# Gate logits computed with standing weights and a moving token tile, in the cross-attention stage of a one-layer decoder kernel

## The chip, the cores and the metric

The program runs on one core of a Trainium2 chip. The metric is the device time of one execution in microseconds; less is better. The core has a matrix engine (TensorE, in the profile PE, with its weight loads as PEld), VectorE (DVE), ScalarE (ACT), GpSimd (POOL) and a queue engine for transfers (SyncE, SP). Each engine works through its own instructions in program order; semaphores join them.

## The reference, cut to what matters

One decoder layer over 2048 tokens of width 1024: token mixing, cross-attention over 256 memory tokens with 4 heads, and a mixture of experts. This case touches the end of the cross-attention part, where the residual stream `x` is normalised and the experts' gate reads it:

```python
x = x + memory_cross_attention(rmsnorm(x, norm_cross), rmsnorm(mem, norm_mem), ...)
h = rmsnorm(x, norm_moe)
g_logits = h @ w_group + b_group      # 2048 x 4
e_logits = h @ w_router + b_router    # 2048 x 32
# top-1 group by g_logits, then top-2 experts of that group by e_logits
```

The 36 logits of a token decide which experts it goes to, so they are computed to float32 accuracy, not to the reduced accuracy of the chip's fast 4-byte mode (`F32R`). Large products elsewhere in the kernel split both operands into a high and a low `F32R` part and take three products (`split_product`, L62 to 66).

## The kernel before, in words

`attend_memory` handles the cross-attention of all 16 tiles of 128 tokens. It first folds the projections into the keys and values (8 steps, `wq_t`, `sk_hi`, `sk_lo`, `vo_hi`, `vo_lo`); then it runs rounds `b` from -2 to 16, software-pipelined over the tiles. The loop in the middle holds two rounds in its body and turns four times; the first five and the last six rounds are written out. `there(b, lag)` says whether tile `b + lag` exists.

In a round `b` TensorE does, in this order: the scores of tile b+1 (`z_ps`, 48 matmuls of 512 columns, L64 to 66); the transposes of the normalised tile b-1 (`turn_hm`, into `s_ps`, L1587); the transposes of tile b+2 of the input (`turn_x`, into `h_ps`); the output of tile b (`x_ps`, 48 matmuls); the gate logits of tile b-1 (L1668); the transposes of the attention weights of tile b+1 (`s_ps`, L1587). In round 15 (`is_last`) `turn_hm` stands behind the output instead of ahead of it. The logits of before are 8 float32 matmuls in which the transposed token tile `hm_t` (128 x 128) is the standing operand and the gate's weights `w_logit` (128 x 36) move:

```python
pe.wait_ge(mt_out, b)
for r in range(rows):
    last = nc.tensor.matmul(h_ps[:, 0, 0:n_logit], hm_t[:, r], w_logit[:, r], ...)
last.then_inc(logit_done, 1)
```

ScalarE in a round: high part of the transposed attention weights (L1458), square of the residual for the norm (L1464), square of a later input tile (L1426), copy of the transposed tile `hm_t` (L1471), high part of the input (L1432), four exponentials (L1480).

VectorE in a round: residual add (L1539, into `x2_sb`), low part of the attention weights (L1544, `p_lo`), norm of tile b-1 (L1548, L1552, which writes `hm_sb`), norm of a later tile (L1490, L1492), row maximum (L1558), low part of the input (L1503), softmax division (L1565, L1568), and last the logits' bias add (L1578), which writes `logits`. In round 15 `picks.choose(nc, link, 0, 14)` (L1711 on) stands ahead of that bias add: it chooses group and experts for tiles 0 to 13. In round 16 `picks.choose(nc, link, 14, 1)` does so for tile 14, again ahead of the bias add. The last tile is chosen for in the next stage, which begins after a barrier of all engines (`Scope.close`, L28 to 31).

Of the kernel before, what the change touches and what calls it, by code (L numbers as in the profile page):

```python
# [14 lines left out]
P = 128  # L15
# [1233 lines left out]
class CrossLoads:  # L1249


    def __init__(self, s, w_q, w_o):
        self.w_q, self.w_o = w_q, w_o
        self.xs = s.sbuf("cross_xs", [P, 2, w_q.shape[1]])
        self.work = s.sbuf("cross_work", [P, 4, w_q.shape[1]])
        self.wq_loaded = [s.sem(f"wq_loaded{i}") for i in range(2)]
        self.wo_loaded = [s.sem(f"wo_loaded{i}") for i in range(2)]
# [14 lines left out]

def attend_memory(nc, x1, gain_q, ahead, key_t, value_t, gain_moe, w_group, w_router, b_group, b_router,
                  ident, half, x2, hm, logits, consts):
# [13 lines left out]
    with ExitStack() as stack:  # L1288
# [14 lines left out]
        p_sb, x2_sb, hm_sb = work[:, 0], work[:, 1], work[:, 2]  # L1303
        hm_t = work[:, 3].rearrange("p (r t) -> p r t", t=P)
        p_hi, p_lo = p_parts[:, 0], p_parts[:, 1]
# [12 lines left out]
                 "res_loaded x2_stored hm_stored squared meaned rooted h_done ht_done hh_done hl_done scored maxed negated exped "  # L1318
                 "inverted p_done tp_done ph_done pl_done xo_done added m_squared m_meaned m_rooted hm_done tm_done mt_out "
                 "logit_done logit_out picked")  # L1320
        (consts_loaded, gains_loaded, wt_done, wt_act, wt_dve, sk_done, sk_cut, sk_ready, vo_done, vo_cut, vo_ready,
         res_loaded, x2_stored, hm_stored, squared, meaned, rooted, h_done, ht_done, hh_done, hl_done, scored, maxed, negated, exped,
         inverted, p_done, tp_done, ph_done, pl_done, xo_done, added, m_squared, m_meaned, m_rooted, hm_done, tm_done, mt_out,
         logit_done, logit_out, picked) = (s.sem(n) for n in names.split())
        halves = [slice(0, rows // 2), slice(rows // 2, rows)]
# [16 lines left out]
        def is_first(b):  # L1342

            return isinstance(b, int) and b == -2

        def there(b, lag):

            return not isinstance(b, int) or 0 <= b + lag < tiles

        with nc.Block() as block:  # L1350
# [44 lines left out]
            @block.gpsimd  # L1395
            def _(pool):
                def root(t):
                    pool.wait_ge(meaned, t + 1)
                    nc.gpsimd.tensor_tensor(stat[:, 2:3], stat[:, 1:2], half[:, 0:1], ALU.pow).then_inc(rooted, 1)

                root(0)

                def step(b, slot):
                    if there(b, -1):
                        pool.wait_ge(m_meaned, b)
                        nc.gpsimd.tensor_tensor(m_stat[:, 2:3], m_stat[:, 1:2], half[:, 0:1], ALU.pow).then_inc(m_rooted, 1)
                    if there(b, 3):
                        root(b + 3)

                rounds(pool, step)  # L1410

            @block.scalar
            def _(act):
# [39 lines left out]
                def step(b, slot):  # L1453
# [11 lines left out]
                    if there(b, 3):  # L1465
                        square(b + 3, 1 - slot, (b + 3) // 2 + 1)
                    if there(b, -1):
                        act.wait_ge(tm_done, b)
                        wait_past(act, logit_done, b - 1)
                        for cut in halves:  # L1470
                            last = nc.scalar.copy(hm_t[:, cut], s_ps[:, cut])  # L1471
                        last.then_inc(mt_out, 1)
                    if there(b, 2) and not is_first(b):
                        high_x(b + 2)
                    if there(b, 1):
                        act.wait_ge(negated, b + 2)
                        wait_past(act, tp_done, b + 1)
                        for h in range(heads):
                            cut = slice(h * slots, (h + 1) * slots)
                            last = nc.scalar.activation(p_sb[:, cut], z_ps[:, cut], ACT.Exp,  # L1480
                                                        bias=soft_stat[:, 1, h:h + 1], scale=scale, accum_out=soft_stat[:, 2, h:h + 1])
                        last.then_inc(exped, 1)

                rounds(act, step)

            @block.vector
            def _(dve):
# [46 lines left out]
                def step(b, slot):  # L1534
# [19 lines left out]
                    if there(b, 3):  # L1554
                        norm(b + 3, 1 - slot)
                    if there(b, 1):
                        dve.wait_ge(scored, b + 2)
                        nc.vector.tensor_reduce(soft_stat[:, 0], z_ps[:].rearrange("p (h m) -> p h m", h=heads), AX.X, ALU.max).then_inc(maxed, 1)  # L1558
                        dve.wait_ge(maxed, b + 2)
                        nc.vector.tensor_scalar(soft_stat[:, 1], soft_stat[:, 0], -scale, None, ALU.mult).then_inc(negated, 1)  # L1560
                    if there(b, 2) and not is_first(b):
                        low_x(b + 2)
                    if there(b, 1):
                        dve.wait_ge(exped, b + 2)
# [11 lines left out]
                    if there(b, -1):  # L1576
                        dve.wait_ge(logit_done, b)
                        nc.vector.tensor_tensor(logits[:, bass.ds(b - 1, 1), :], h_ps[:, 0:1, 0:n_logit],  # L1578
                                                b_logit[:].rearrange("p (o c) -> p o c", o=1), ALU.add).then_inc(logit_out, 1)
# [4 lines left out]
            def _(pe):  # L1584
# [16 lines left out]
                for n in range(rows):  # L1601
# [22 lines left out]
                    last.then_inc(vo_done, 1)  # L1624
                pe.wait_ge(consts_loaded, 80)

# [6 lines left out]
                def step(b, slot):  # L1633
# [27 lines left out]
                    if there(b, -1):  # L1661
                        pe.wait_ge(mt_out, b)
                        if there(b, 2):
# [3 lines left out]
                        for r in range(rows):  # L1667
                            last = nc.tensor.matmul(h_ps[:, 0, 0:n_logit], hm_t[:, r], w_logit[:, r], start=r == 0, stop=r == rows - 1)  # L1668
                        last.then_inc(logit_done, 1)
                    if there(b, 1):  # L1670
# [3 lines left out]
                        pe.wait_ge(p_done, b + 2)  # L1674
                        wait_past(pe, mt_out, b)
                        transposes(s_ps, p_sb, tp_done)

                rounds(pe, step)
# [698 lines left out]
def build_trunk(nc, x, mem, norm_mix, w_in, v_norm, w_spatial, b_spatial, out_norm_a, out_norm_b, w_out, norm_cross, norm_mem,  # L2377
# [16 lines left out]
    with ExitStack() as stack:  # L2394
# [8 lines left out]
        with ExitStack() as before_moe:  # L2403
# [15 lines left out]
            with ExitStack() as crossing:  # L2419
                c = Scope(nc, crossing, "kv")  # L2420
                key_t, value_t = c.sbuf("key_t", [P, rows, slots]), c.sbuf("value_t", [P, rows, slots])
                ahead = CrossLoads(c, w_xq[0], w_xo[0])
                project_memory(nc, memory, w_xk[0], w_xv[0], ident[:], consts, key_t, value_t, ahead, tiles)
                picks = attend_memory(nc, x1, norm_cross[0], ahead, key_t, value_t, norm_moe[0], w_group[0], w_router[0],
                              b_group[0], b_router[0], ident[:], half, x2, hm, logits, consts)
# [27 lines left out]
```

## Time and profile before

| what | value |
|---|---|
| median of 3 runs | 2663.56 us (2662.22 to 2663.6) |
| profiled execution, first to last instruction | 2659.8 us |
| TensorE busy | 2536.7 us (95% of the span) |
| VectorE busy | 1478.0 us (56%) |
| ScalarE busy | 1283.6 us (48%) |
| GpSimd busy | 602.4 us (23%) |
| mean granted TensorE clock | 0.981 |
| the rounds in the middle | 1300 to 1662 us of the span |
| the last two rounds | 1662.7 to 1696.1 us |

The span of the profiled execution is 3.8 us below the median of the timed runs; this is what lies around the first and last instruction. Busy times of TensorE overlap from one instruction to the next, so what a matmul costs in a stream is read from the distance of two starts, not from its own duration. The granted clock is 1.00 at 2.4 GHz and 0.50 at 1.2 GHz.

### The profile page before, as it was taken

Reading aid. Unit: us, or ns where it says so; the run is one execution under the profiler, and the core shown is the slowest. Engines: PE = TensorE matmul, PEld = TensorE weight load, DVE = VectorE, ACT = ScalarE, POOL = GpSimd, SP = SyncE. Lnnn points to the kernel's source line nnn. Section 1 sums busy time; section 2 is a strip of 40 time slices with the busy share of each in tenths; the row PEclk is TensorE's granted clock in tenths of the full one; section 3 lists DMA queues with packets and bytes.
Section 4 is the critical chain, followed back from the end, with each engine's and each line's share of the span. In section 5 each row is a group of like instructions: output and inputs, shape, how many; then the busy total and the mean of one; then the engine's idle time right before and its main releaser. Section 6 shows DMA issues by size and latency. Waiting matters only on the chain. (4 is left out here: it accounts for less than half of the span.)

```text
span 2659.8 us, 44805 instructions
## 1 busy us (share of the span) xinstructions
PE 2536.7 (95%) x14537; PEld 2053.6 (77%) x14539; DVE 1478.0 (56%) x1943; ACT 1283.6 (48%) x2286; POOL 602.4 (23%) x650
## 2 busy tenths in 40 slices
PE   9999999999999999989999999799999999999991
PEld 7888888676666678886888888688877888888881
DVE  5221344698888964444333332667888655565643
ACT  5221211698898931133222222346787645465543
POOL 0000011577777710000000000012222221121223
PEclk9999999999999999999999999799999999999996
DMA  7433240313201033243122121538999765576757
GB/s 267 167 119 127 75 166 25 100 45 144 65 18 45 2 127 111 99 152 112 62 82 85 73 87 48 200 130 326 386 379 367 267 220 200 191 279 205 253 161 271
DMA packets 141439, 414.83 MB, mean 156 GB/s; under 512 B 22016, under 2 KB 30720, under 8 KB 140288
## 3 DMA queue, kind: packets, MB, share of 16 engines
q1 hardware_dynamic: 125040, 371.15, 37.5%
q0 software_dynamic: 13968, 33.59, 5.3%
q10 hardware_dynamic: 2304, 8.39, 0.8%
q8 instruction: 81, 1.33, 0.2%
q14 instruction: 46, 0.38, 0.0%
HBM read 338.60 MB, written 91.75 MB: 162 GB/s over the span
## 5 line engine op out<-in xcount | busy, mean ns | idle before, releaser
L673 POOL TENSOR_TENSOR stick_weight<-stick_weight,stick_left 128x512 f32<-128x512 f32 (+3 forms) x320 | 327.8, 1038 | 126.9 <-DVE stick_left L805 122.4
L1820 DVE TENSOR_TENSOR moe_w_lo<-moe_w_lo_raw,moe_w_hi (+1 forms) x256 | 298.2, 1220 | 59.6 <-ACT moe_w_hi L1816 53.3
L1816 ACT CAST moe_w_hi<-moe_w_lo_raw (+1 forms) x256 | 255.7, 1052 | 48.2 <-DMA moe_w_lo_raw<-in_w 24.8
L805 DVE TENSOR_TENSOR_SCAN stick_left<-stick_z_ps,stick_left,stick_any_row 128x512 f32<-128x512 f32 x192 | 240.2, 1274 | 35.4 <-ACT stick_z_ps L768 35.1
L766 ACT ACTIVATE stick_weight<-stick_z_ps 128x512 f32<-128x512 f32 (+3 forms) x320 | 173.9, 543 | 32.8 <-PE stick_z_ps L715 21.1
L728 PE MATMUL stick_t_ps<-all_ident,stick_weight 128*128 128x128 f32 x1088 | 165.1, 281 | 19.0 <-ACT stick_weight_t L775 9.2
L768 ACT ACTIVATE stick_z_ps<-stick_z_ps 128x512 f32<-128x512 f32 (+3 forms) x320 | 165.7, 518 | 10.2
L728 PEld LDWEIGHTS stick_t_ps<-all_ident,stick_weight 128*128 128x128 f32 x1088 | 115.9, 141 | 70.0 <-issue 46.2
L64 PE MATMUL exp_g_ps<-moe_w_hi,exp_x_hi 128*128 x376 | 153.1, 407 | 7.1 <-DVE exp_x_lo L2224 7.1
L1831 POOL DMA_INDIRECT moe_xg<-hm_scratch,moe_now x50 | 62.4, 1247 | 412.6 <-PE exp_x_ps L2260 273.7
L64 PE MATMUL proj_z_ps<-proj_w_hi,proj_h_hi 128*128 128x512 f32 x384 | 151.9, 396 | 2.5 <-DVE proj_h_lo L392 2.5
L64 PE MATMUL exp_y_ps<-moe_w_hi,exp_h_hi 128*128 128x512 f32 x376 | 152.1, 405 | 2.3 <-DVE exp_h_lo L2244 2.3
L2248 DVE TENSOR_TENSOR moe_w_lo<-moe_w_lo_raw,moe_w_hi 128x1024 f32 (+1 forms) x128 | 148.2, 1218 | 9.8 <-ACT moe_w_hi L2210 9.8
L66 PE MATMUL proj_z_ps<-proj_w_hi,proj_h_lo 128*128 128x512 f32 x384 | 150.3, 391 | 0.0
L65 PE MATMUL proj_z_ps<-proj_w_lo,proj_h_hi 128*128 128x512 f32 x384 | 150.2, 391 | 0.0
L65 PE MATMUL exp_g_ps<-moe_w_lo,exp_x_hi 128*128 x376 | 148.9, 396 | 0.0
L66 PE MATMUL exp_g_ps<-moe_w_hi,exp_x_lo 128*128 x376 | 148.8, 396 | 0.0
L66 PE MATMUL exp_u_ps<-moe_w_hi,exp_x_lo 128*128 x376 | 148.5, 395 | 0.0
L66 PE MATMUL exp_y_ps<-moe_w_hi,exp_h_lo 128*128 128x512 f32 x376 | 148.5, 395 | 0.0
L64 PE MATMUL exp_u_ps<-moe_w_hi,exp_x_hi 128*128 x376 | 148.3, 394 | 0.0
L65 PE MATMUL exp_u_ps<-moe_w_lo,exp_x_hi 128*128 x376 | 148.3, 394 | 0.0
L65 PE MATMUL exp_y_ps<-moe_w_lo,exp_h_hi 128*128 x376 | 148.2, 394 | 0.0
(290 smaller groups left out, 5820.2 us busy)
## 6 DMA issues: line engine op xcount, KB each, us to landing
moe_w_lo_raw<-in_w SPq DMA_DIRECT2D x384, 512.0 KB, 13.0
proj_w_lo_raw<-in_w_in SPq DMA_DIRECT2D x40, 256.0 KB, 6.3
proj_xs<-in_x SPq DMA_DIRECT2D x16, 512.0 KB, 4.3
qt_scratch<-proj_qk_out SPq DMA_DIRECT2D x16, 512.0 KB, 2.8
kt_scratch<-proj_qk_out SPq DMA_DIRECT2D x16, 512.0 KB, 2.7
mix_q<-qt_scratch SPq DMA_DIRECT2D x16, 512.0 KB, 3.8
mix_out_xs<-in_x SPq DMA_DIRECT2D x16, 512.0 KB, 4.4
x_scratch<-mix_out_xs SPq DMA_DIRECT2D x16, 512.0 KB, 3.0
```

The lines of the kernel that those rows point to most:

```text
L64: pe.matmul(out, left_hi, right_hi, start=first, stop=False)
L65: pe.matmul(out, left_hi, right_lo, start=False, stop=False)
L66: return pe.matmul(out, left_lo, right_hi, start=False, stop=last)
L673: nc.gpsimd.tensor_tensor(taken, taken, after, ALU.mult).then_inc(weight_done, 1)
L728: last = nc.tensor.transpose(t_ps[:, n % 2, b], weight[:, n % W_SLOTS, b * P:(b + 1) * P], ident)
L766: nc.scalar.activation(weight[:, n % W_SLOTS, 0:keys], z, ACT.Sigmoid).then_inc(take_done, 1)
L768: nc.scalar.activation(z, z, ACT.Sigmoid, scale=-1.0).then_inc(leave_done, 1)
L805: nc.vector.tensor_tensor_scan(row[:, c * BANK:c * BANK + keys][:, ::-1], back, any_row[:, 0:keys], start, ALU.mult, ALU.bypass).then_inc( ...
L1816: nc.scalar.copy(self.w13_hi[:, self.w13_at(e, i)], self.w13_raw[:, self.w13_at(e, i)]).then_inc(self.w13_cut, 1)
L1820: ops.tensor_tensor(self.w13_lo[:, self.w13_at(e, i)], self.w13_raw[:, self.w13_at(e, i)], as_f32(self.w13_hi[:, self.w13_at(e, i)]), ALU. ...
L1831: nc.gpsimd.indirect_dma_start(out=self.xg[:], out_offset=None, in_=self.hm, in_offset=bass.IndirectOffsetOnAxis(ap=self.now[:].bitcast(U3 ...
L2248: nc.vector.tensor_tensor(w2_lo[:, w2_at(e, i)], w2_raw[:, w2_at(e, i)], as_f32(w2_hi[:, i]), ALU.subtract).then_inc(w2_ready, 1)
```

## The change

The gate's weights become the standing operand and the token tile moves. For that the weights are split once into a high and a low `F32R` part that stand side by side (`w_cut`, 72 columns), the transposed tile is split into a high and a low part (`hm_parts`, ScalarE and VectorE), and 8 `F32R` matmuls move both parts at once (256 columns) and give all four partial products, transposed (`h_ps[0:72, 1:3]`). ScalarE copies these to `parts`, as its last step of the round; then two float32 matmuls against a 72 x 36 matrix of two stacked identities (`both_parts`, set up by GpSimd ahead of everything) add the products up and turn them back to tokens by logits, where the bias add finds them. The two matmuls stand behind the transposes of the attention weights, as TensorE's last step of the round.

On VectorE the new low part stands between `low_x` and the softmax division, so ahead of `picks.choose` in rounds 15 and 16. The weights are split in round -1: ScalarE waits there for the constants and makes the high part, VectorE the low part. TensorE's wait for the constants ahead of the rounds goes, one for `both_parts` takes its place. `hm_parts` lies over the keys' buffer, `w_cut` and `parts` over the fourth slice of `work`, where `hm_t` was. The core of the diff:

```diff
@@ GpSimd, ahead of the rounds
+                nc.gpsimd.memset(both_parts[:], 0.0).then_inc(both_set, 1)
+                for part in range(2):
+                    pool.wait_ge(both_set, part + 1)
+                    nc.gpsimd.affine_select(out=both_parts[:], in_=both_parts[:], compare_op=ALU.not_equal, fill=1.0, base=-part * n_logit,
+                                            pattern=[[-1, n_logit]], channel_multiplier=1).then_inc(both_set, 1)
@@ ScalarE, a round
+                    if is_early(b):
+                        act.wait_ge(consts_loaded, 80)
+                        nc.scalar.copy(w_cut[:, :, 0:n_logit], w_logit[:]).then_inc(w_hi_cut, 1)
                     if there(b, -1):
                         act.wait_ge(tm_done, b)
                         wait_past(act, logit_done, b - 1)
                         for cut in halves:
-                            last = nc.scalar.copy(hm_t[:, cut], s_ps[:, cut])
+                            last = nc.scalar.copy(hm_parts[:, cut, 0], s_ps[:, cut])
                         last.then_inc(mt_out, 1)
...
+                    if there(b, -1):
+                        act.wait_ge(logit_done, b)
+                        wait_past(act, parts_added, b - 1)
+                        nc.scalar.copy(parts[:], h_ps[0:2 * n_logit, 1:3]).then_inc(parts_out, 1)
@@ VectorE, a round
+                    if is_early(b):
+                        dve.wait_ge(w_hi_cut, 1)
+                        nc.vector.tensor_tensor(w_cut[:, :, n_logit:], w_logit[:], as_f32(w_cut[:, :, 0:n_logit]), ALU.subtract).then_inc(w_cut_done, 1)
...
                     if there(b, 2) and not is_first(b):
                         low_x(b + 2)
+                    if there(b, -1):
+                        dve.wait_ge(mt_out, b)
+                        wait_past(dve, logit_done, b - 1)
+                        for cut in halves:
+                            last = nc.vector.tensor_tensor(hm_parts[:, cut, 1], s_ps[:, cut], as_f32(hm_parts[:, cut, 0]), ALU.subtract)
+                        last.then_inc(ml_out, 1)
...
                     if there(b, -1):
-                        dve.wait_ge(logit_done, b)
+                        dve.wait_ge(parts_added, b)
                         nc.vector.tensor_tensor(logits[:, bass.ds(b - 1, 1), :], h_ps[:, 0:1, 0:n_logit],
@@ TensorE
-                pe.wait_ge(consts_loaded, 80)
+                pe.wait_ge(both_set, 3)
...
-                        pe.wait_ge(mt_out, b)
+                        if isinstance(b, int) and b == 1:
+                            pe.wait_ge(w_cut_done, 1)
+                        pe.wait_ge(ml_out, b)
...
-                            last = nc.tensor.matmul(h_ps[:, 0, 0:n_logit], hm_t[:, r], w_logit[:, r], start=r == 0, stop=r == rows - 1)
+                            last = nc.tensor.matmul(h_ps[0:2 * n_logit, 1:3], w_cut[:, r], hm_parts[:, r], start=r == 0, stop=r == rows - 1)
                         last.then_inc(logit_done, 1)
...
                         pe.wait_ge(p_done, b + 2)
-                        wait_past(pe, mt_out, b)
+                        wait_past(pe, ml_out, b)
                         transposes(s_ps, p_sb, tp_done)
+                    if there(b, -1):
+                        pe.wait_ge(parts_out, b)
+                        for part in range(2):
+                            last = nc.tensor.matmul(h_ps[:, 0, 0:n_logit], parts[:, part], both_parts[:], start=part == 0, stop=part == 1)
+                        last.then_inc(parts_added, 1)
```

## Rows read from the trace of the kernel before

**Rows 1.** The page's first line: span and instructions.

```profile
span 2659.8 us, 44805 instructions
```

**Rows 2.** Busy time by stretch; behind POOL: granted clock, DMA share, GB/s.

```profile
1300.00:1662.00 362.00, 362.00 (x1872) 308.17 (x1871) 120.26 (x199) 94.87 (x242) 14.28 (x26) 1.00 0.21 76
```

**Rows 3.** Timeline of a round's end: start, length, engine, line, what, idle before.

```profile
1504.50 1.87 PE L1668 MATMUL cross_h_ps<-cross_w_logit,kv_cross_work 128*128 128x36 f32 x16
...
1506.20 1.07 PE L1587 MATMUL cross_s_ps<-all_ident,kv_cross_work 128*128 128x128 f32 x8
1506.52 0.20 DVE L1578 TENSOR_TENSOR pre_logits<-cross_h_ps,cross_b_logit 128x36 f32 x1 [8.27 <-PE cross_h_ps L1668]
...
1507.03 0.48 PE L64 MATMUL cross_z_ps<-cross_sk_hi,cross_h_hi 128*128 128x512 f32 x1
1507.04 1.29 DVE L1539 TENSOR_TENSOR kv_cross_work<-cross_x_ps,kv_cross_work 128x512 f32<-128x512 f32 x2 [0.33 <-issue]
```

**Rows 4.** Timeline of TensorE where the memory tokens are projected (256 columns).

```profile
1150.01 0.28 PE L64 MATMUL mem_z_ps<-mem_m_hi,mem_w_hi 128*128 128x256 f32 x1
1150.13 0.28 PE L65 MATMUL mem_z_ps<-mem_m_lo,mem_w_hi 128*128 128x256 f32 x1
```

**Rows 5.** Timeline of TensorE in token mixing (weights of 64 columns).

```profile
701.71 1.09 PE L743 MATMUL stick_o_ps<-stick_weight_t,stick_v_other 128*64 128x128 f32 x16
```

**Rows 6.** Groups of instructions on ScalarE by form: count, busy us, mean ns.

```profile
L775 ACT COPY stick_weight_t<-stick_t_ps 128x256 f32<-128x256 f32 x16 | 6.1, 380 | 0.0
```

**Rows 7.** Timeline of VectorE late in the round that ends with rows 3.

```profile
1494.99 1.29 DVE L1503 TENSOR_TENSOR cross_h_lo<-cross_h_ps,cross_h_hi 128x512 fp32r<-128x512 f32 x2 [1.53 <-ACT cross_h_hi L1432]
...
1497.03 1.23 DVE L1568 TENSOR_TENSOR kv_cross_work<-kv_cross_work,cross_soft_stat 128x1024 f32<-128x1024 f32 x1
```

**Rows 8.** Timeline of ScalarE in round -1.

```profile
1268.45 1.07 ACT L1432 CAST cross_h_hi<-cross_h_ps 128x512 fp32r<-128x512 f32 x2 [5.83 <-PE cross_h_ps L1587]
```

**Rows 9.** Timeline of VectorE in round -1.

```profile
1267.58 1.23 DVE L1558 TENSOR_REDUCE cross_soft_stat<-cross_z_ps 128x4 f32<-128x1024 f32 x1 [3.36 <-PE cross_z_ps L66]
```

**Rows 10.** Timeline of VectorE, rounds 15 and 16 and the next stage.

```profile
1668.12 0.21 DVE L1724 TENSOR_REDUCE cross_pick_g_max<-pre_logits 128x14 f32<-128x56 f32 x1
...
1678.39 0.39 DVE L1744 TENSOR_TENSOR cross_pick_both<-cross_pick_pick 128x448 bf16<-128x448 bf16 x1
1684.26 0.20 DVE L1578 TENSOR_TENSOR pre_logits<-cross_h_ps,cross_b_logit 128x36 f32<-128x36 f32 x1 [5.48 <-PE cross_h_ps L1668]
1684.37 1.28 DVE L1539 TENSOR_TENSOR kv_cross_work<-cross_x_ps,kv_cross_work 128x512 f32<-128x512 f32 x2
...
1688.89 0.15 DVE L1724 TENSOR_REDUCE cross_pick_g_max<-pre_logits 128x1 f32<-128x4 f32 x1
...
1693.17 0.17 DVE L1744 TENSOR_TENSOR cross_pick_both<-cross_pick_pick 128x32 bf16<-128x32 bf16 x1
1695.90 0.20 DVE L1578 TENSOR_TENSOR pre_logits<-cross_h_ps,cross_b_logit 128x36 f32<-128x36 f32 x1 [2.56 <-PE cross_h_ps L1668]
1697.52 0.16 DVE L1724 TENSOR_REDUCE cross_pick_g_max<-pre_logits 128x1 f32<-128x4 f32 x1 [1.42 <-PEq L31]
```

**Rows 11.** Timeline of TensorE, rounds 15 and 16.

```profile
1666.25 0.80 PE L64 MATMUL cross_x_ps<-cross_vo_hi,cross_p_parts 128*128 128x512 f32 x1 [2.49 <-DVE cross_p_parts L1544]
...
1679.75 0.40 PE L66 MATMUL cross_x_ps<-cross_vo_hi,cross_p_parts 128*128 128x512 f32 x1
1679.98 1.04 PE L1587 MATMUL cross_s_ps<-all_ident,kv_cross_work 128*128 128x128 f32 x8
1682.18 1.98 PE L1668 MATMUL cross_h_ps<-cross_w_logit,kv_cross_work 128*128 128x36 f32 x16 [1.16 <-ACT kv_cross_work L1471]
1689.03 1.97 PE L1587 MATMUL cross_s_ps<-all_ident,kv_cross_work 128*128 128x128 f32 x8 [4.87 <-DVE kv_cross_work L1552]
1692.16 3.63 PE L1668 MATMUL cross_h_ps<-cross_w_logit,kv_cross_work 128*128 128x36 f32 x16 [1.16 <-ACT kv_cross_work L1471]
```

**Rows 12.** Busy time by stretch in round 15, columns as in rows 2.

```profile
1666.00:1670.00 4.00, 3.75 (x9) 2.98 (x10) 3.10 (x11) 0.00 (x0) 0.55 (x1) 0.50 0.35 137
```

More of the change, by code:

```diff
@@ L1254, in __init__ @@
         self.xs = s.sbuf("cross_xs", [P, 2, w_q.shape[1]])
+        self.work_at = s.next_at()
         self.work = s.sbuf("cross_work", [P, 4, w_q.shape[1]])
@@ L1270, in load_first, with attend_memory @@
             self.load_wo(sp, n)
-def attend_memory(nc, x1, gain_q, ahead, key_t, value_t, gain_moe, w_group, w_router, b_group, b_router,
+def attend_memory(nc, x1, gain_q, ahead, key_t, value_t, key_at, gain_moe, w_group, w_router, b_group, b_router,
                   ident, half, x2, hm, logits, consts):
@@ L1303, in attend_memory @@
         p_sb, x2_sb, hm_sb = work[:, 0], work[:, 1], work[:, 2]
-        hm_t = work[:, 3].rearrange("p (r t) -> p r t", t=P)
+        hm_parts = s.over("hm_parts", [P, rows, 2, P], F32R, key_at)
+        w_cut = s.over("w_cut", [P, rows, 2 * n_logit], F32R, ahead.work_at + 4 * 3 * width)
+        parts = s.over("parts", [2 * n_logit, 2, P], F32, ahead.work_at + 4 * (3 * width + 2 * rows * n_logit))
+        both_parts = s.sbuf("both_parts", [2 * n_logit, n_logit])
         p_hi, p_lo = p_parts[:, 0], p_parts[:, 1]
@@ L1318, in attend_memory @@
                  "res_loaded x2_stored hm_stored squared meaned rooted h_done ht_done hh_done hl_done scored maxed negated exped "
-                 "inverted p_done tp_done ph_done pl_done xo_done added m_squared m_meaned m_rooted hm_done tm_done mt_out "
-                 "logit_done logit_out picked")
+                 "inverted p_done tp_done ph_done pl_done xo_done added m_squared m_meaned m_rooted hm_done tm_done mt_out ml_out "
+                 "logit_done logit_out picked both_set w_hi_cut w_cut_done parts_out parts_added")
         (consts_loaded, gains_loaded, wt_done, wt_act, wt_dve, sk_done, sk_cut, sk_ready, vo_done, vo_cut, vo_ready,
          res_loaded, x2_stored, hm_stored, squared, meaned, rooted, h_done, ht_done, hh_done, hl_done, scored, maxed, negated, exped,
-         inverted, p_done, tp_done, ph_done, pl_done, xo_done, added, m_squared, m_meaned, m_rooted, hm_done, tm_done, mt_out,
-         logit_done, logit_out, picked) = (s.sem(n) for n in names.split())
+         inverted, p_done, tp_done, ph_done, pl_done, xo_done, added, m_squared, m_meaned, m_rooted, hm_done, tm_done, mt_out, ml_out,
+         logit_done, logit_out, picked, both_set, w_hi_cut, w_cut_done, parts_out, parts_added) = (s.sem(n) for n in names.split())
         halves = [slice(0, rows // 2), slice(rows // 2, rows)]
@@ L1344, in is_first, with is_early @@
             return isinstance(b, int) and b == -2
+        def is_early(b):
+            return isinstance(b, int) and b == -1
         def there(b, lag):
@@ L2420, in build_trunk @@
                 c = Scope(nc, crossing, "kv")
+                key_at = c.next_at()
                 key_t, value_t = c.sbuf("key_t", [P, rows, slots]), c.sbuf("value_t", [P, rows, slots])
@@ L2423, in build_trunk @@
                 project_memory(nc, memory, w_xk[0], w_xv[0], ident[:], consts, key_t, value_t, ahead, tiles)
-                picks = attend_memory(nc, x1, norm_cross[0], ahead, key_t, value_t, norm_moe[0], w_group[0], w_router[0],
+                picks = attend_memory(nc, x1, norm_cross[0], ahead, key_t, value_t, key_at, norm_moe[0], w_group[0], w_router[0],
                               b_group[0], b_router[0], ident[:], half, x2, hm, logits, consts)
```

## The prediction

> **What bounds the kernel now.** I read the first line of the page for the span [rows 1], then the busy time by stretch, then timelines of single rounds engine by engine. In the middle rounds TensorE is busy for 362.00 of 362 us at full clock [rows 2]: whatever shortens its stream there shortens the kernel by as much, and nothing that the other engines do counts until TensorE waits for it. At the end of the stage it is the other way round. In rounds 15 and 16 TensorE idles 2.49, 1.16, 4.87 and 1.16 us [rows 11], and the end is set by a chain that goes from engine to engine. All later work starts behind a barrier: the next stage's first VectorE instruction comes 1.42 us after the last bias add [rows 10], and what delays that add delays everything behind it.
>
> So the change has two prices: what a middle round gains on TensorE, and what the last two rounds lose or gain on the chain.
>
> **A middle round on TensorE.** The old logits start at 1504.50 and the transposes behind them at 1506.20 [rows 3]: 1.70 us for 16 records (each float32 matmul leaves two), 0.106 us each. The new eight move 256 columns in the fast mode. Their nearest row is the projection of the memory tokens, the same mode and width, with starts 0.12 us apart [rows 4]: 8 x 0.12 = 0.96 us. Their weights have 72 columns and not 128; 16 matmuls with weights of 64 columns take 1.09 us in all, so some 0.07 us each at most [rows 5], and such loads don't slow the stream. The two float32 matmuls that add up the parts have weights of 128 columns and 36 moving ones, as the old ones have: 4 records x 0.106 = 0.42 us. New sum 1.38 us, against 1.70: a middle round gets 0.32 us shorter, if TensorE never waits.
>
> Bounds: were each of the twelve new records at 0.106 us or below, down to the 0.07 us of [rows 5] for the four small ones, the round would gain 1.70 - 0.85 - 0.28 = 0.57 us; with a wait as below it gains nothing. I take 0.32, since the rows for it have the same shape and mode.
>
> The FP8 and Floating Point Precision page of the Trainium skill (TensorE Precision Notes) says that true float32 takes four passes through the array, which speaks against this change: an old block that paid for its moved columns alone would take 8 x 36 x 4 columns, 0.48 us at 2.4 GHz as an estimate, and the new eight with their 2048 columns 0.85 us. By that rule each round would lose. The row disagrees: the old block takes 1.70 us [rows 3]. The page TensorE: Matmul & The Clock Gate of the Trainium skill (LDWEIGHTS) has the reason: a weight load takes its columns divided by 1.2 ns, 107 ns for 128 columns, and the 0.106 us of a record agrees.
>
> **Does TensorE wait for the parts?** Counted from the start of the eight: the last starts at 0.84 and ends 0.28 later [rows 4], at 1.12. ScalarE is done with its exponentials long before. The old logits end at 1506.37 (1504.50 + 1.87) and release VectorE's bias add at 1506.52 [rows 3], 0.15 us later; with as much the copy starts at 1.27. It is 72 x 256 from PSUM; the 128 x 256 copy takes 0.38 us [rows 6]. The parts are there at 1.65, or at 1.55 if the release takes less. TensorE's transposes start at 0.96 and take until the next matmul 0.83 us (1506.20 to 1507.03 [rows 3]): it comes to its wait at 1.79. The cover is 0.15 to 0.25 us, and it must hold TensorE's own release too. It is thin, and where the loop turns (four times) an engine that has run dry (VectorE in [rows 3]) needs 0.33 us to issue again. If the cover fails, TensorE loses what is missing in each of 14 rounds; 0.3 us each is my bound, worked out as a copy that starts or ends half a copy late plus a share of that issue time.
>
> **The other engines in a middle round.** VectorE gets a low part of the size of `h_lo`: 1.29 us [rows 7]. It stands ahead of the division, which ended at 1498.26 and would end by 1499.6 [rows 7]; TensorE takes its result at 1506.20 and the low part itself at 1504.50 [rows 3]. More than 5 us of cover each, free. The bias add now comes behind the parts, so the residual add starts 0.2 to 0.5 us later than at 1507.04, and what follows from it (norm, transposes, both stores and the next load of the residual by SP's queue) is needed a good 10 us later. Free. ScalarE's cast in place of its copy has the same size, and ScalarE waits for TensorE at the round's end anyway.
>
> **The start.** ScalarE idles 5.83 us in round -1 ahead of its high part, VectorE 3.36 us ahead of its maximum [rows 8, 9]; the split of 288 elements a partition is less than the 0.38 us of [rows 6] on each. GpSimd's three instructions run while the eight folding steps do, and nothing asks for them before the rounds. The constants' new waiter comes later than the old one. All of it zero; without the cover it would be about 1 us once.
>
> **Rounds 14 to 16, where the order of VectorE decides.** Round 14 gains on TensorE, but round 15 begins with TensorE waiting 2.49 us for `p_lo` [rows 11], which VectorE makes behind the bias add and the residual add. These start behind the parts now, 0.3 us earlier than before less the longer way over ScalarE. I count half a round's gain, 0.15 us. Middle gain: 13 x 0.32 + 0.15 = 4.3 us.
>
> Round 15. Before, VectorE goes straight from its norm into the choice for 14 tiles, 1668.12 to 1678.78, while TensorE computes the output of tile 15; it is done 5.48 us before the logits come [rows 10]. Now the new low part stands ahead of the choice. It waits for ScalarE's copy of the transposed tile, and in this round the transposes come behind the output, at 1679.98 [rows 11]; that copy releases the old logits at 1682.18 [rows 11]. So VectorE stands still through the whole output of tile 15 and then does in a row:
> - low part 1682.18 to 1683.47 (1.29 us [rows 7])
> - choice for 14 tiles 10.66 us, to 1694.13 [rows 10]
> - bias add, and 0.11 us behind it the residual add of tile 15, at 1694.27 instead of 1684.37 [rows 10].
>
> That is 9.9 us. TensorE's logits and ScalarE's copy lie inside the 10.66 us and cost nothing.
>
> Round 16. From the residual add to the transposed copy nothing changes: the copy releases the old logits at 1692.16 in the old time [rows 11]. Before, the choice for tile 14 ran beside the transposes and the copy, 1688.89 to 1693.34, and the bias add came at 1695.90 [rows 10]. Now: low part 1692.16 to 1693.45, choice 4.45 us to 1697.9, bias add at once, if the parts are added by then. TensorE is at the half clock there (8 transposes take 1.97 us instead of 1.07 [rows 3, 11]): eight matmuls at 0.24 us from 1693.5 end by 1695.7, copy to 1696.1, four records at 3.63 / 16 = 0.23 us [rows 11] end by 1697.2. In time, by 0.7 us. Loss 2.0 us.
>
> **Sum.** -4.3 + 9.9 + 2.0 = +7.6 us on a span of 2659.8, so 2667.4; with the 3.8 us around it, 2671.2 us against the median of 2663.56, which is 0.29% more. Behind the barrier the work is the same and is only shifted.
>
> **The rivals.**
> - *The choice is not held back* (the other side). If VectorE could choose during the output of tile 15, only the longer logit chain would count: about 1.5 us in round 15 (low part 1.29, shorter matmuls, copy, four records) and 1.3 us in round 16, less the 4.3 (2663.56 + 2.8 - 4.3): 2662.1 us, no change. It decides on one point, whether the wait for the copy of tile 14 is fulfilled before 1668; the order of the code and [rows 11] say no. 6 in 100.
> - *TensorE waits for ScalarE's copy each round.* The cover of 0.2 us fails and the 0.32 us are gone: 2671.2 + 4.3 = 2675.5. For it speaks that TensorE's queue runs dry with each wait that comes late; against it the sum above. 14 in 100.
> - *The clock.* The output of tile 15 took 13.73 us (1666.25 to 1679.98), where 48 matmuls at full clock, 0.23 us each [rows 11], take 11.0, for TensorE fell to the half clock behind its 2.49 us of idling [rows 11, 12]. Timing shifts by some us here and the fall can be missed, or last longer: -2.7 us, so 2668.5, or +2 us. The first 10 in 100, the second within my range.
> - *Moved columns set the price*, not loads: the eight move 2048 columns where the old moved 288. At 0.106 us a record the trace bears this out in nothing; were the new eight to cost the old 1.70 us and the four records more, a round would lose 0.42 us, 14 rounds 5.9, and the time would be 2681. The four-pass rule would lead there. 1 in 100.
>
> **How the numbers follow.** The forecast as it stands has 69 in 100. Under 0.2% (5.3 us, about what a measurement of this kernel can tell from no change) lie the first rival, most of the missed clock fall and a small part of the forecast where a round gains near the bound of 0.57 us: 18 in 100. Faster by over 0.2% needs the first rival and the upper bound together: 2. Slower: 80. The range runs from the missed clock fall less a little, 2667.5, to the failed cover, 2675.8.
>
> **What would show it.** In the trace of the changed kernel: the eight at 0.12 us and the four at 0.106; the distance of two rounds shorter by 0.3 us; TensorE still without a gap before the loop ends; VectorE's wait for the copy in round 15 of about 14 us, and L1724's wide form starting after the transposes of tile 14 and not at 1668 less the gain; the bias add of tile 15 about 8 us later than before against the span's start. A gap ahead of the two small matmuls in every round would show the second rival. The prediction is wrong if the wide choice starts before the output of tile 15 is done, or if a round's gain is not between 0 and 0.57 us.

## The result and the profile after

The changed kernel takes 2666.97 us (median of 21 runs, 2664.31 to 2669.4); before, measured again beside it, takes 2662.22 us (median of 21, 2660.07 to 2663.6). The ratio is 1.0017 with a 95% interval of 1.0011 to 1.0023: the change costs 2.9 to 6.1 us, some 4.7. I had forecast 7.6 us more and a time of 2671.2 with a range from 2667.5. The measured time lies 0.5 us below that range.

The first lines of the page after, which answer to [rows 1]:

```profile
span 2666.3 us, 44763 instructions
...
PE 2530.0 (95%) x14474; PEld 2045.6 (77%) x14475; DVE 1496.4 (56%) x1976; ACT 1291.6 (48%) x2303; POOL 608.1 (23%) x653
```

TensorE is busy for 6.7 us less than before (2536.7 us), in part because one block ran at a higher clock, as shown below, and the span is 6.5 us longer. So the lost time is not work of TensorE.

The timeline at the end of a middle round (the one ahead of the round in [rows 3]), and busy time by stretch for the middle rounds as in [rows 2]:

```profile
1478.08 1.11 PE L1699 MATMUL cross_h_ps<-cross_hm_parts,cross_w_cut 128*72 128x256 f32 x8
...
1479.02 1.03 PE L1616 MATMUL cross_s_ps<-all_ident,kv_cross_work 128*128 128x128 f32 x8
1479.22 0.37 ACT L1502 COPY cross_parts<-cross_h_ps 72x256 f32<-72x256 f32 x1 [8.86 <-PE cross_h_ps L1699]
...
1479.79 0.53 PEld L1711 LDWEIGHTS cross_h_ps<-cross_both_parts,cross_parts 72*128 72x128 f32 x4
1479.89 0.53 PE L1711 MATMUL cross_h_ps<-cross_both_parts,cross_parts 72*128 72x36 f32 x4
...
1480.26 0.48 PE L64 MATMUL cross_z_ps<-cross_sk_hi,cross_h_hi 128*128 128x512 f32 x1
...
1480.57 0.20 DVE L1607 TENSOR_TENSOR pre_logits<-cross_h_ps,cross_b_logit 128x36 f32 x1 [8.19 <-PE cross_h_ps L1711]
```

```profile
1290.00:1658.00 368.00, 368.00 (x1867) 311.95 (x1866) 140.22 (x234) 103.86 (x263) 14.32 (x26) 1.00 0.21 76
```

From the start of the logits to the next scores TensorE takes 2.18 us (1478.08 to 1480.26) where it took 2.53 before: 0.94 for the eight, 0.87 for the transposes, 0.37 for the four small records. ScalarE's copy runs wholly beside the transposes, and TensorE has no gap in 368 us. One round lasts 25.77 us (logits of tile 0 at 1323.06 and of tile 13 at 1658.04, 13 rounds) instead of 26.16 (1320.91 to 1660.99).

The timelines of VectorE and of TensorE in rounds 15 and 16, which answer to [rows 10] and [rows 11]:

```profile
1663.85 1.28 DVE L1572 SCALAR_TENSOR_TENSOR kv_cross_work<-kv_cross_work,cross_m_stat,cross_m_gains 128x1024 f32<-128x1024 f32 x1 [0.66 <-POOL cross_m_stat L1419]
1676.27 1.29 DVE L1590 TENSOR_TENSOR cross_hm_parts<-cross_s_ps,cross_hm_parts 128x512 fp32r<-128x512 f32 x2 [11.14 <-ACT cross_hm_parts L1487]
1677.48 0.20 DVE L1760 TENSOR_REDUCE cross_pick_g_max<-pre_logits 128x14 f32<-128x56 f32 x1
...
1687.73 0.39 DVE L1780 TENSOR_TENSOR cross_pick_both<-cross_pick_pick 128x448 bf16<-128x448 bf16 x1
1688.15 0.19 DVE L1607 TENSOR_TENSOR pre_logits<-cross_h_ps,cross_b_logit 128x36 f32<-128x36 f32 x1
1688.27 1.28 DVE L1559 TENSOR_TENSOR kv_cross_work<-cross_x_ps,kv_cross_work 128x512 f32<-128x512 f32 x2
...
1696.02 1.29 DVE L1590 TENSOR_TENSOR cross_hm_parts<-cross_s_ps,cross_hm_parts 128x512 fp32r<-128x512 f32 x2 [3.16 <-ACT cross_hm_parts L1487]
1697.23 0.15 DVE L1760 TENSOR_REDUCE cross_pick_g_max<-pre_logits 128x1 f32<-128x4 f32 x1
...
1701.50 0.17 DVE L1780 TENSOR_TENSOR cross_pick_both<-cross_pick_pick 128x32 bf16<-128x32 bf16 x1
1701.71 0.20 DVE L1607 TENSOR_TENSOR pre_logits<-cross_h_ps,cross_b_logit 128x36 f32<-128x36 f32 x1
1703.37 0.16 DVE L1760 TENSOR_REDUCE cross_pick_g_max<-pre_logits 128x1 f32<-128x4 f32 x1 [1.47 <-PEq L31]
```

```profile
1663.07 0.50 PE L64 MATMUL cross_x_ps<-cross_vo_hi,cross_p_parts 128*128 128x512 f32 x1 [2.68 <-DVE cross_p_parts L1564]
...
1674.09 1.04 PE L1616 MATMUL cross_s_ps<-all_ident,kv_cross_work 128*128 128x128 f32 x8
1677.62 1.32 PE L1699 MATMUL cross_h_ps<-cross_hm_parts,cross_w_cut 128*72 128x256 f32 x8 [2.49 <-DVE cross_hm_parts L1590]
1679.40 1.07 PE L1711 MATMUL cross_h_ps<-cross_both_parts,cross_parts 72*128 72x36 f32 x4 [0.46 <-ACT cross_parts L1502]
1692.91 1.97 PE L1616 MATMUL cross_s_ps<-all_ident,kv_cross_work 128*128 128x128 f32 x8 [12.45 <-DVE kv_cross_work L1572]
```

The reader should see VectorE's 11.14 us of idling ahead of its low part, while TensorE computes the output of tile 15, and only then the choice for 14 tiles. The bias add at 1688.15 comes straight behind the choice, with no wait: its logits had been there since about 1680.5. TensorE pays for it with 12.45 us ahead of the last tile's transposes.

The two stages laid side by side, in us, from the first transposes of an input tile (1252.10 us in before, 1254.10 in the changed kernel), each piece from the first to the next mark of its own trace:

| piece of the stage | before | after | difference | forecast |
|---|---|---|---|---|
| first transposes to output of tile 15 | 414.15 | 408.97 | -5.18 | -4.3 |
| output of tile 15 (48 matmuls) | 13.73 | 11.02 | -2.71 | 0 |
| its end to the residual add of tile 15 | 4.39 | 14.18 | +9.79 | +9.9 |
| residual add to the last bias add | 11.53 | 13.44 | +1.91 | +2.0 |
| last bias add to the next stage | 1.62 | 1.66 | +0.04 | 0 |
| sum | 445.42 | 449.27 | +3.85 | +7.6 |

The two prices of the last rounds came out to 0.1 us. What was off is the gain, by 0.9 us, and a piece that I had left unchanged: the output of tile 15 ran at full clock where it had been at the half clock for its first 6 us. The remaining 2.65 us between the two spans lie in other stages, where nothing was changed: 2.0 ahead of this one and 0.7 behind it. The start of the stage alone lies anywhere from 1251.55 to 1256.22 us in the 14 traces of all kernels here.

### The profile page after: what moved, and what is told of

Read it like the earlier page. It is cut to its first block and busy times, and to the rows that moved or that the text cites. A ratio compares the mean times of both kernels' runs of the same rounds, so it can differ in the third digit from the quotient of the medians.

```text
span 2666.3 us, 44763 instructions
## 1 busy us (share of the span) xinstructions
PE 2530.0 (95%) x14474; PEld 2045.6 (77%) x14475; DVE 1496.4 (56%) x1976; ACT 1291.6 (48%) x2303; POOL 608.1 (23%) x653
```

## The experiments

My theory: VectorE's order in rounds 15 and 16 makes the loss, a middle round gains 0.39 us, and the clock in the output of tile 15 blurs the sum. The rivals: the longer way of the logits makes the loss; or the two terms are right and something else explains why the total is smaller. All ratios are to the kernel before, timed beside each run on the same chip.

**Order undone, in both rounds (e1) and in round 15 alone (e2).**

The five lines of the low part are put into a function `low_hm(b)`; `late(b)` is true for rounds 15 and 16 in e1, for round 15 in e2.

```diff
-                    if there(b, -1):
+                    if there(b, -1) and not late(b):
                         low_hm(b)
...
                         picks.choose(nc, link, tiles - 2, 1)
+                    if late(b):
+                        low_hm(b)
```

> The changed kernel, with VectorE's low part put behind the choice of experts in rounds 15 and 16. If VectorE's order is the loss, the wide choice runs again during the output of tile 15, the residual add of tile 15 moves from 1688.3 to about 1680.7 us of the changed trace, and round 16 gives back another 0.7 us: 8.3 us less than the changed kernel, so 3.6 us less than before, ratio 0.9986. If instead the longer way of the logits (low part, ScalarE's copy, the two extra matmuls) is the loss, no more than 1 us comes back and the ratio stays near 1.0015.

Measured: 2659.65 us, ratio 0.9991 (0.9982 to 1.0). VectorE in its trace:

```profile
1663.05 0.20 DVE L1769 TENSOR_REDUCE cross_pick_g_max<-pre_logits 128x14 f32<-128x56 f32 x1
1673.30 0.39 DVE L1789 TENSOR_TENSOR cross_pick_both<-cross_pick_pick 128x448 bf16<-128x448 bf16 x1
1675.93 1.29 DVE L1534 TENSOR_TENSOR cross_hm_parts<-cross_s_ps,cross_hm_parts 128x512 fp32r<-128x512 f32 x2 [2.24 <-ACT cross_hm_parts L1491]
1680.00 0.20 DVE L1616 TENSOR_TENSOR pre_logits<-cross_h_ps,cross_b_logit 128x36 f32<-128x36 f32 x1 [2.78 <-PE cross_h_ps L1720]
1680.11 1.28 DVE L1570 TENSOR_TENSOR kv_cross_work<-cross_x_ps,kv_cross_work 128x512 f32<-128x512 f32 x2
```

The wide choice is back under the output of tile 15, and the residual add comes 6.42 us behind that output's end (1673.69) instead of 14.18. That returns 7.8 us where the changed kernel lost 9.8. The 2.0 us that stay are the longer way of the logits (low part, copy, adding matmuls), for which the first rival of the prediction had put 1.5. The whole run came out at 0.9991 where I had expected 0.9986. Round 16 went the other way than I had expected: from residual add to last bias add 13.88 us, 0.44 more than in the changed kernel. The choice for one tile ends at 1689.06, and the low part, now behind it, starts later than ScalarE's copy would have let it. I had reckoned only the case in which the choice is the last to end.

> The changed kernel, with the low part behind the choice in round 15 alone. If the wide choice of 14 tiles is the main loss, 7.6 us come back and ratio to before is about 0.9989; round 16 then keeps its 0.7 us. If the loss were spread evenly over both rounds, only half of it would come back, ratio about 1.0002.

Measured: 2658.99 us, 0.9992 (0.9983 to 1.0001). Round 15 alone gives back all that the order costs; the trace has 6.39 us from the end of tile 15's output to the residual add and 13.45 us in round 16.

**Order alone, without the new gate (e3).** Before, with one line more in each of two places:

```diff
                     if is_last(b):
                         dve.wait_ge(logit_out, tiles - 2)
+                        dve.wait_ge(mt_out, b)
                         picks.choose(nc, link, 0, tiles - 2)
                     if isinstance(b, int) and b == tiles:
                         dve.wait_ge(logit_out, tiles - 1)
+                        dve.wait_ge(mt_out, b)
                         picks.choose(nc, link, tiles - 2, 1)
```

> The kernel before, with nothing of the gate changed: only a wait of VectorE for ScalarE's copy of the transposed tile ahead of both choices. If order alone makes the loss, the wide choice starts at about 1682.2 us, the residual add of tile 15 comes 8.65 us later, and round 16 adds 0.75 us: 9.4 us slower, ratio 1.0035. If the loss needs the new work, this run equals before.

Measured: 2671.57 us, 1.0039 (1.0025 to 1.0052).

```profile
1682.64 0.21 DVE L1726 TENSOR_REDUCE cross_pick_g_max<-pre_logits 128x14 f32<-128x56 f32 x1 [14.03 <-ACT kv_cross_work L1471]
1692.91 0.39 DVE L1746 TENSOR_TENSOR cross_pick_both<-cross_pick_pick 128x448 bf16<-128x448 bf16 x1
1693.33 0.20 DVE L1580 TENSOR_TENSOR pre_logits<-cross_h_ps,cross_b_logit 128x36 f32<-128x36 f32 x1
1693.44 1.28 DVE L1539 TENSOR_TENSOR kv_cross_work<-cross_x_ps,kv_cross_work 128x512 f32<-128x512 f32 x2
```

A wait of 14.03 us ahead of the wide choice, with not one instruction of the new gate in the kernel, costs as much as foreseen: in the trace round 15 loses 8.66 us and round 16 0.80, against 8.65 and 0.75. This and e1 settle the main point from both sides: the order makes 7.8 of the 9.8 us in round 15, and it does so without the new gate too.

**Cover of ScalarE's copy taken away (e6).** The two adding matmuls stand ahead of the transposes of the attention weights:

```diff
                         last.then_inc(logit_done, 1)
+                    if there(b, -1):
+                        pe.wait_ge(parts_out, b)
+                        for part in range(2):
+                            last = nc.tensor.matmul(h_ps[:, 0, 0:n_logit], parts[:, part], both_parts[:], start=part == 0, stop=part == 1)
+                        last.then_inc(parts_added, 1)
                     if there(b, 1):
...
                         transposes(s_ps, p_sb, tp_done)
-                    if there(b, -1):
-                        pe.wait_ge(parts_out, b)
-                        for part in range(2):
-                            last = nc.tensor.matmul(h_ps[:, 0, 0:n_logit], parts[:, part], both_parts[:], start=part == 0, stop=part == 1)
-                        last.then_inc(parts_added, 1)
```

> The changed kernel, with the two adding matmuls ahead of the transposes of the attention weights, so that nothing covers ScalarE's copy. If the copy was hidden, TensorE now waits 0.6 us in each of 14 rounds: 8.8 us more than the changed kernel, ratio to before about 1.005. If the copy was not hidden in the changed kernel, moving it changes little, ratio about 1.002.

Measured: 2675.74 us, 1.0053 (1.0039 to 1.0067), 9 us more than the changed kernel. The end of a round:

```profile
1640.45 1.10 PE L1699 MATMUL cross_h_ps<-cross_hm_parts,cross_w_cut 128*72 128x256 f32 x8
1641.59 0.37 ACT L1502 COPY cross_parts<-cross_h_ps 72x256 f32<-72x256 f32 x1 [8.86 <-PE cross_h_ps L1699]
1642.01 0.52 PEld L1704 LDWEIGHTS cross_h_ps<-cross_both_parts,cross_parts 72*128 72x128 f32 x4 [0.71 <-ACT cross_parts L1502]
1642.01 0.64 PE L1704 MATMUL cross_h_ps<-cross_both_parts,cross_parts 72*128 72x36 f32 x4 [0.46 <-ACT cross_parts L1502]
1642.48 1.07 PE L1616 MATMUL cross_s_ps<-all_ident,kv_cross_work 128*128 128x128 f32 x8
```

The parts reach TensorE 1.56 us after the eight began. In the changed kernel the load of the parts as weights starts at 1.71 (1478.08 to 1479.79) and the matmul at 1.81. The cover was there, and 0.15 us thick, or 0.25 counted to the matmul.

**The clock in the output of tile 15 (e0, e4, e5, and three more traces, e9 to e11).** The filling:

```diff
                         if isinstance(b, int) and b == 0:
                             pe.wait_ge(vo_ready, rows)
+                        if is_last(b):
+                            keep_busy(nc.tensor, z_ps[:, 0:P], ident, 11)
                         pe.wait_ge(pl_done, b + 1)
```

> The changed kernel once more, as the neighbour of the next runs: ratio 1.0017 as measured. If the output of tile 15 falls to the half clock in some executions and not in others, its trace may show this block at 13.7 us here, where the first trace shows 11.0.

Measured: 2666.22 us, 1.0017 (1.0008 to 1.0026).

> The kernel before, with 11 identity matmuls (some 2.5 us, results unused) in TensorE's gap ahead of the output of tile 15. If the half clock behind that gap costs its 2.7 us in every execution of before, this is 2.7 us faster, ratio 0.9990. If the fall happens in none or few, no change.

Measured: 2659.62 us, 0.9994 (0.9985 to 1.0003).

> The changed kernel with the same filling. If the changed kernel never falls to the half clock there, as its trace shows, this equals the changed kernel, ratio 1.0017, and the forecast's shortfall is explained by the clock. If it falls there as often as before does, both fillings give the same gain, and the clock does not explain the shortfall.

Measured: 2666.12 us, 1.0016 (1.0007 to 1.0025).

> One more trace of the changed kernel, for the output of tile 15. If the clock there differs between executions of one kernel, it takes anything from 11.0 to 13.7 us; if it is fixed by where the block lies, 11.0 or 12.6 us as in the two traces so far.

> One more trace of the kernel before, for the same block: 13.7 us if its place fixes the clock (as in the first trace and in the run with the wait alone), anything from 11.0 to 13.7 us if chance does.

> As the look at the changed kernel before: 11.0 to 12.7 us for the output of tile 15 if the new gate shortens the stretch at the half clock, 13.7 us if this is chance alone.

The three runs e9 to e11, one execution each, took 2665.89, 2662.97 and 2665.13 us. The block in question, from its first matmul to the transposes behind it, in every trace that has it unfilled: with the old gate 13.73 (before), 13.72 (e3) and 12.64 us (e10); with the new gate 11.02 (after), 12.62 (e0), 12.62 (e9), 12.63 (e11) and 12.63 to 12.66 (e1, e2, e6). Filled, it takes 11.02 us (e4, e5). The granted clock shows why. Busy time by stretch of before:

```profile
1663.80:1666.20 2.40, 0.00 (x0) 0.00 (x0) 1.78 (x4) 2.12 (x4) 0.00 (x0) 0.80 0.46 184
1666.25:1672.20 5.95, 5.95 (x14) 4.70 (x15) 4.95 (x13) 0.00 (x0) 0.55 (x1) 0.51 0.52 187
```

and of e0, from the idle time on:

```profile
1658.80:1661.30 2.50, 0.00 (x0) 0.00 (x0) 2.48 (x6) 1.74 (x4) 0.00 (x0) 1.00 0.16 64
1661.33:1661.90 0.57, 0.57 (x3) 0.49 (x4) 0.12 (x1) 0.00 (x0) 0.37 (x1) 1.00 0.99 402
1662.00:1665.40 3.40, 3.40 (x10) 2.63 (x9) 1.28 (x1) 0.00 (x0) 0.08 (x1) 0.50 0.42 158
1665.50:1673.90 8.40, 8.40 (x38) 6.90 (x37) 0.00 (x0) 0.00 (x0) 0.00 (x0) 1.00 0.21 69
```

TensorE idles 2.49 us in before and 2.68 in e0. In before the clock fell to 1.2 GHz during the idle time, and the first 13 matmuls ran at it. In e0 it fell when the matmuls had begun again, and some eight were slow. In the changed kernel's first trace it did not fall (granted clock 1.00 throughout). So one kernel shows more than one outcome, 11.0 or 12.6 us with the new gate and 12.6 or 13.7 with the old. The first trace of the changed kernel flatters it by 1.6 us against its three others, and the trace of before that I predicted from was the dearer of its two. So the place of the block does not fix the clock for either kernel, as I had offered. The mean of three unfilled traces with the old gate is 13.4 us and that of seven with the new gate 12.4; whether this 1.0 us is chance, three against seven traces cannot say. The timings of e4 and e5 cannot either: the interval of e4 holds both its forecast and no change, and that of e5 both 1.0017 and the 1 us less that its trace would give.

Without that block the stage is steady: 431.69 and 431.72 us in the two traces of before, 438.12 to 438.30 in the four of the changed kernel. That is +6.5 us, the price of the change without this block. It lies above the whole measured interval of 2.9 to 6.1 us, so the block or the other stages give something back; which of them, and how much, the runs don't settle.

The barrier behind the stage doesn't wipe out the clock either. From the next stage's first instruction to the first product with the experts' weights the changed kernel's first trace takes 43.28 us, at a mean granted clock of 0.85, where before takes 41.29 at 0.89 and e0, e9 and e11 take 41.17 to 41.28 at 0.87 to 0.88. From that first instruction to the end of the span kernels with either gate overlap, 961.0 to 962.5 us with the old gate and 960.2 to 963.8 with the new one.

**Putting it together (e7, e8).** e1 with the filling, and with the bias add of tile 14 moved behind the norm of tile 15, so that the residual add of tile 15 doesn't queue behind it:

```diff
-                    if there(b, -1):
+                    if there(b, -1) and not is_last(b):
                         add_bias(b)
...
                     if isinstance(b, int) and b == tiles:
+                        add_bias(tiles - 1)
                         dve.wait_ge(logit_out, tiles - 1)
                         picks.choose(nc, link, tiles - 2, 1)
```

> The changed kernel with the low part behind the choice in rounds 15 and 16, the gap filled, and the bias add of tile 14 behind the norm of tile 15, so that the residual add of tile 15 does not wait for the logits of tile 14. 8.3 us from the order, 2.9 us from the residual add, up to 1.4 us from the clock: 12 us less than the changed kernel, ratio to before 0.997. If the residual add was not what the end hangs on, it equals the run with the order alone, 0.9986.

Measured: 2656.14 us, 0.9979 (0.997 to 0.9988): faster than both kernels, though not by all of the 12 us. In the trace the residual add comes 3.44 us behind the output of tile 15 instead of 6.42 in e1, as foreseen. But round 16 takes 15.24 us instead of 13.88, 1.1 of them because ScalarE's square of the residual comes behind its copy of the parts of tile 14 in its order and now has to wait for it, and VectorE waits for the square 2.32 us instead of 1.22.

e8 puts the low part of round 16 ahead of the choice again and the bias add of tile 14 ahead of both (against e7):

```diff
-            return isinstance(b, int) and b >= tiles - 1
+            return isinstance(b, int) and b == tiles - 1
...
+                    if isinstance(b, int) and b == tiles:
+                        add_bias(tiles - 1)
...
-                        add_bias(tiles - 1)
```

> The run with order, filling and residual add moved, with one thing put back: in round 16 the low part stands ahead of the choice again, and the bias add of tile 14 ahead of both. By the traces of the two order runs, round 16 took 13.88 us from residual add to last bias add with the low part behind the choice and 13.45 us with it ahead, so 0.4 to 0.7 us less than the run before, ratio to before about 0.9976. If my reckoning of e1 was right, it is 0.7 us slower instead.

Measured: 2656.52 us, 0.9976 (0.9967 to 0.9985).

```profile
1679.60 1.28 DVE L1575 TENSOR_TENSOR kv_cross_work<-cross_x_ps,kv_cross_work 128x512 f32<-128x512 f32 x2
1684.40 0.19 DVE L1532 TENSOR_TENSOR pre_logits<-cross_h_ps,cross_b_logit 128x36 f32<-128x36 f32 x1
1687.65 1.29 DVE L1539 TENSOR_TENSOR cross_hm_parts<-cross_s_ps,cross_hm_parts 128x512 fp32r<-128x512 f32 x2 [3.06 <-ACT cross_hm_parts L1491]
...
1693.35 0.20 DVE L1532 TENSOR_TENSOR pre_logits<-cross_h_ps,cross_b_logit 128x36 f32<-128x36 f32 x1
```

Round 16 takes 13.75 us from residual add to last bias add, against 15.24 in e7, 1.5 us better and not 0.7. The two timings don't tell them apart. With the order put right, the gap filled and the residual add moved up, the kernel with the new gate is 0.24% faster than before, where the change as made costs 0.17%. That is not the gate's own gain: the filling and the earlier residual add might serve the old gate as well, and no run has both with it. The order alone (e1, e2) gives 0.9991 and 0.9992, with intervals that reach 1.

## Why the prediction was wrong in size and right in kind

Two terms of the sum were mis-sized. The gain of the middle rounds was put at 4.3 us and measured 5.18, and the output of tile 15 was put at no change and measured 2.71 us less in the first pair of traces. The mechanism of the loss held.

- **What bounds where:** right. TensorE has no gap in the middle rounds after the change either, and the end hangs on the chain through VectorE.
- **The middle round on TensorE:** the sign is right, the size too small. The term "a middle round gets 0.32 us shorter" measured 0.39. The four small records took 0.37 us and not 0.42, and the eight 0.94 and not 0.96; the transposes took 0.04 more. The block accounts for 0.35 of the 0.39; the other 0.04 lies in the two runs of 48 matmuls (the scores took 11.02 us before and 11.00 after, the output 11.01 and 10.99), and why stays open. Over the stretch up to the output of tile 15 that is 5.18 us instead of 4.3, and it holds in all six unfilled traces of the two kernels (414.15 and 414.18 against 408.82 to 409.01).
- **Does TensorE wait for the parts:** no, as forecast. The copy starts at 1.14 and is done at 1.51 (I had 1.27 and 1.65), so the cover is 0.15 us to the weight load, at the lower end of my 0.15 to 0.25, and e6 shows what it is worth.
- **The start:** the two splits took 0.42 and 0.45 us, more than I had put as the bound, and lay under the scores as foreseen.
- **Rounds 15 and 16:** right to 0.1 us each, 9.79 for 9.9 and 1.91 for 2.0. e3 makes the loss without the gate, e1 and e2 take it away with the gate in place.
- **The clock:** this term failed. The sum took the half clock behind TensorE's idle time as given, 13.73 us as in the one trace, and had its absence as a rival with 10 in 100. It is neither there nor absent: 11.0 to 13.7 us, by where the fall comes. It also shortened VectorE's wait in round 15 to 11.14 us where I had said about 14. With the mean of the traces, 1.0 us less under the new gate, and the 0.9 us of the middle rounds the forecast would have been 5.7 us, inside the measured interval of 2.9 to 6.1. But that the 1.0 us is a steady difference is not shown: filling the gap brought the changed kernel no measurable time (1.0016 for 1.0017).
- **The reference point:** I added 7.6 us to a median of three runs, 2663.56. The median of 21 is 2662.22. Of the 4.2 us by which 2671.2 missed 2666.97, 1.3 come from there and 2.9 from the two terms above and the scatter. With 2662.22 in its place the range would have begun at 2666.2 and held the measured time. The 3.8 us between span and median are not what lies around the first and last instruction, as I wrote: every timed execution here is 1.7 to 1.8 us longer than its own span, and the other 2 us say that the traced execution was a short one.
- **Behind the barrier:** that the work is only shifted holds within the scatter of the spans, not for each trace: the next stage's start took 2.0 us more in the changed kernel's first trace.
- **The rivals:** the choice was held back, TensorE didn't wait for ScalarE, moved columns didn't set the price. The four-pass rule of the Trainium skill (FP8 and Floating Point Precision, TensorE Precision Notes) would have made a round dearer; the trace has it 0.39 us cheaper.

The chances were off with the size: I gave 18 in 100 to a change under 0.2%, and 0.17% is one.

## What to carry to other kernels

When a new step is put into an engine's fixed order, look at each round that is not like the others: here the step was free in 14 rounds and held back 10.66 us of unrelated work in the one round whose producer comes late. A saving of 0.39 us in a round is soon eaten by one such place, so move the late-fed step behind the work that is ready. And a piece that stands behind idle time of TensorE should enter a sum with both of its clocks.

## What the runs showed of the hardware

- TensorE idled for 2.68 us ahead of the same 48 matmuls, and in four traces of the changed kernel these took 11.02, 12.62, 12.62 and 12.63 us. In the ten unfilled traces of all kernels (idle time 2.49 or 2.68 us) the fall to 1.2 GHz came during the idle time in two, behind the first two to six matmuls in seven, and not at all in one. 11 small matmuls in the gap kept the block at 11.0 to 11.1 us in all four traces that have them (e4, e5, e7, e8).
- The length of a weight load's record doesn't go by its columns alone: 141 ns for the 72 columns of the new gate and 192 for the 128 of the old, but 140 for the 128 of the transposes (L1616). The 256-column matmuls behind them start 0.12 us apart with 72 columns of weights as with 128.
- The small float32 matmuls leave records 0.11 us apart, with weights of 72 rows as with 128. Only the first distance of a group differs: 0.03 to 0.04 us where it follows other matmuls without a gap, 0.13 behind a wait. That is why the four took 0.37 us in the changed kernel and 0.47 in e6 (1642.01 to 1642.48), and why 4 x 0.106 was a little too much.
